# Seven half-size products in place of eight in the gate and up projections of two feed-forwards

## The chip, the core and the metric

The kernel runs on one core of a Trainium2 chip. The metric is the device time in microseconds of one execution, the median of several. Engines are named as the profile names them: PE is TensorE (PEld its weight loads), DVE is VectorE, ACT is ScalarE, POOL is GpSimd, SP issues the weight transfers.

## The reference

Three transformer blocks over 512 tokens of width 1024, in float32, one after the other. The first two end in a feed-forward of hidden width 2816:

```python
def swiglu(h, w_gate, w_up, w_down):
    return (jax.nn.silu(h @ w_gate) * (h @ w_up)) @ w_down
# per layer:
h = rmsnorm(x, ffn_norm[layer])
x = x + swiglu(h, ffn_w_gate[layer], ffn_w_up[layer], ffn_w_down[layer])
```

The third block ends in another feed-forward (`ffn2`) with a convolution, which the change leaves alone.

## The kernel before

All is held with features on the 128 partitions and the 512 tokens along the free axis. Float32 products are made from three fp32r matmuls: a value is split into a high part (ScalarE copies it to fp32r) and a low part (VectorE subtracts the high part from the value), and hi x hi, hi x lo and lo x hi are added up in PSUM. The activations stand split in `XH` and `XL` (8 tiles of 128 features each), multiplied by the norm's gain but not by `rstd`.

Weights come in units of 1 MB: 1024 input features by 256 hidden features, a gate unit and an up unit in turn. SP loads a unit into one of two raw buffers `w_raw` as soon as the low part of the unit two before is made (`w_lo_ready`). ScalarE makes `w_hi` once TensorE has read that buffer's previous weights, VectorE makes `w_lo`, and TensorE (`pair`, line 2893) makes the two 128-feature tiles of the unit, each of 8 x 3 matmuls of 512 columns, in banks 4 and 5 for gate and 2 and 3 for up. A gate and an up unit are one round; there are 11 rounds. The first unit of a feed-forward is made by `first_pair` (line 2839), which follows the norm tile by tile; after it a matmul with ones (line 2410) sums the squares, and ScalarE makes `rstd` (lines 1084 and 1085). VectorE multiplies each tile by `rstd` (lines 1885 and 1900) on its way out of PSUM to `gp` or `ut`, ScalarE applies silu (line 1300), and VectorE multiplies the two into `hid` (line 1912). The order on each engine is the order of the code; rounds 2 to 10 are a hardware loop on PE, ACT, DVE and SP. Then `first_down` (line 2944) and `down_unit` (line 2926) make the down products from `hid`, split again into high and low, in all eight banks.

Other lines that the text names: 1291, 1311 (high parts of up and gate units), 1870, 1876 (their low parts), 1582 and 1036 (low and high parts of other stages' units), 2450 (`token_tile`, 256 columns, in the attention projections), 1970 (an activation times a gain times `rstd`).

Of the kernel before, what the change touches and what calls it, by code (L numbers as in the profile page):

```python
# [8 lines left out]
F32 = mybir.dt.float32  # L9
# [4 lines left out]
ALU = mybir.AluOpType  # L14
# [73 lines left out]
def alibi_rows():  # L88
# [4 lines left out]
    for h in range(4):  # L93
# [10 lines left out]

# [63 lines left out]
def build(nc, d, out, scratch, stages):  # L168
# [18 lines left out]
    with ExitStack() as ctx:  # L187
# [70 lines left out]
        bias_row = sem("bias_row")  # L258
        bias_row_ready = sem("bias_row_ready")
# [9 lines left out]
        sq_mixed = sem("sq_mixed")  # L269
# [5 lines left out]
        gains_ready = sem("gains_ready")  # L275
# [48 lines left out]
        keys_zeroed = sem("keys_zeroed")  # L324
        sb_sum = sem("sb_sum")
# [5 lines left out]
        rope_arg = sem("rope_arg")  # L331
        rope_ready = sem("rope_ready")
        alibi_loaded = sem("alibi_loaded")
        lam_prod = sem("lam_prod")
# [3 lines left out]
        krope_ready = sem("krope_ready")  # L338
# [106 lines left out]
        early_hi, early_lo = (under_arena[:, at:at + 1024].rearrange("p (a b) -> p a b", b=512) for at in early_at)  # L445

# [168 lines left out]
        down_base = {s: KT * i for i, s in enumerate(ffn_order)}  # L615

# [252 lines left out]
        def _(pool):  # L869
# [30 lines left out]
            pool.wait_ge(bias_row_ready, 1)  # L900
# [115 lines left out]
        def _(act):  # L1016
# [263 lines left out]

            def ffn(s):
# [38 lines left out]
                if s != "ffn2":  # L1320
                    up_high(0)
                reciprocal_root(s if s != "ffn2" else "fpre")
                if s == "ffn2":
                    for k in range(2, KT):
                        turned_kept(k)
                body(0)
                if s == "ffn2":
                    body(1)
                with act.Fori(2 if s == "ffn2" else 1, HT // 2 - 1) as i:
                    up_high(i)  # L1330
                    body(i)
                act.wait_ge(hid_done, h0 + 2)
                ffn_hidden_split(s, u0, 0)
                up_high(HT // 2 - 1, last=True)
                body(HT // 2 - 1)
# [15 lines left out]
                if s == "ffn0":  # L1351
                    act.wait_ge(rope_arg, 1)
                    act.activation(rotab[64:128, :], rotab[64:128, :], ACT.Sin).then_inc(rope_ready, 1)
                    exp_and_log()
                if s == "ffn1":
                    act.wait_ge(lam_prod, 1)
# [15 lines left out]
            def mla():  # L1372
# [18 lines left out]
                for half in range(2):  # L1391
# [20 lines left out]
                    if half == 0:  # L1412
                        act.wait_ge(krope_ready, 1)
# [6 lines left out]
            def mix2():  # L1420
                act.wait_ge(gains_ready, 1)
# [146 lines left out]
        def _(dve):  # L1568
# [160 lines left out]
            def even():  # L1729
# [15 lines left out]
                for u in tok_units("even_qkv"):  # L1745
# [34 lines left out]
                    if j == 0:  # L1780
# [7 lines left out]
                        dve.memset(tabx[32:33, :], 1.0).then_inc(bias_row, 1)  # L1788
# [3 lines left out]
                        dve.tensor_tensor(gain12, vec[:, at:at + KT], vec[:, at2:at2 + KT], ALU.mult).then_inc(gains_ready, 1)  # L1792
# [70 lines left out]
            def ffn(s):  # L1863
# [56 lines left out]
                if s == "ffn2":  # L1920
                    body(1)
# [1439 lines left out]
```

## Time and profile before

| | us |
|---|---|
| median of 3 runs | 1924.94 (1923.69 to 1925.65) |
| span of the profiled execution | 1924.0 |
| PE busy | 1890.1 |
| DVE busy | 999.1 |
| ACT busy | 740.1 |
| gate and up work of the first feed-forward, from its second unit on | 228.53 |
| the same of the second | 228.53 |

The profile comes from one execution, whose span is 1924.0 us from the first to the last instruction. "Busy" of PE counts each matmul up to a modelled end, and neighbouring matmuls overlap in it; the time that one matmul costs in a stream is the time from start to start. The view of the chain of waits gives that, as the length of a run of matmuls and their number. Columns of every view are described where it stands first below.

### The profile page before, as it was taken

The page shows a single profiled execution, that of the slowest core. Times are in us where ns is not written, and L with a number is a line of the kernel's source. Part 1 is how long each engine was busy: PE and PEld are TensorE (multiplying, and loading weights), DVE is VectorE, ACT ScalarE, POOL GpSimd, SP SyncE. Part 2 cuts the span into 40 slices and gives each one's busy share as a digit, 9 for nine tenths or more (in the row PEclk, how much of TensorE's full clock was granted, in tenths as well). Part 3 has the DMA queues.
Part 4 walks back from the last instruction along what each step waited for, and adds up shares of the span by engine and source line. Part 5 has one row for each costly group of instructions (what it writes and reads, how often), then busy time and mean ns, then how long its engine had stood idle before and what let it go on. Part 6 is the DMA issues. An engine that isn't in the chain of part 4 may idle for free.

```text
span 1924.0 us, 26779 instructions
## 1 busy us (share of the span) xinstructions
PE 1890.1 (98%) x10729; PEld 1527.6 (79%) x10729; DVE 999.1 (52%) x1418; ACT 740.1 (38%) x1111; POOL 179.1 (9%) x215
## 2 busy tenths in 40 slices
PE   9999999999999999999999999999999999999998
PEld 7875788888888777788888888777878778888887
DVE  5456453434325686553343434749563566656523
ACT  4247432222224575542222323554342454333322
POOL 1001210000001100010000000303551100000001
PEclk9999999999999999999999999999999999999999
DMA  6310133232322202123223232321120223232321
GB/s 201 105 44 1 50 99 98 87 109 87 105 92 80 72 23 66 45 91 105 91 87 109 88 109 87 100 88 44 24 67 25 88 77 109 87 108 89 107 90 66
DMA packets 137795, 158.74 MB, mean 83 GB/s; under 512 B 15976, under 2 KB 125552, under 8 KB 137712
## 3 DMA queue, kind: packets, MB, share of 16 engines
q1 hardware_dynamic: 136272, 155.01, 25.2%
q0 software_dynamic: 1440, 2.58, 0.5%
q8 instruction: 58, 0.95, 0.2%
q14 instruction: 25, 0.20, 0.0%
HBM read 153.89 MB, written 3.68 MB: 82 GB/s over the span
## 4 chain that ended last, share of the span: by engine, by line
PE 90%; DVE 6%; ACT 2%; issue 1%; DMA 0%; SPq 0%; POOL 0%; ACTq 0%; DVEq 0%
PE bank L2893 35%; PE bank L2926 16%; PE bank L2425 13%; PE bank L2450 3%; PE bank L2980 2%; PE bank L2569 2%; PE bank L2944 2%; PE bank L2839 1%; PE bank L2872 1%; PE bank L2597 1%; PE bank L2688 1%; PE bank L2584 1%; PE bank L2511 1%; PE bank L2541 1%; DVE XL L1589 1%
## 5 line engine op out<-in xcount | busy, mean ns | idle before, releaser
L2893 PE MATMUL bank<-XH,w_hi 128*128 128x512 f32 x992 | 386.8, 390 | 0.7 <-DVE arena L1889 0.7
L2893 PE MATMUL bank<-XL,w_hi 128*128 128x512 f32 x992 | 386.0, 389 | 0.0
L2893 PE MATMUL bank<-XH,w_lo 128*128 128x512 f32 x992 | 385.9, 389 | 0.0
L2893 PEld LDWEIGHTS bank<-XH,w_hi 128*128 128x128 f32 x992 | 186.2, 188 | 39.9 <-DVE arena L1889 0.9
L2893 PEld LDWEIGHTS bank<-XL,w_hi 128*128 128x128 f32 x992 | 186.2, 188 | 39.1 <-issue 0.5
L2893 PEld LDWEIGHTS bank<-XH,w_lo 128*128 128x128 f32 x992 | 186.2, 188 | 38.8
L2425 PE MATMUL bank<-XH,w_hi 128*128 128x512 f32 x448 | 178.7, 399 | 2.5 <-DVE w_lo L1582 2.4
L2425 PE MATMUL bank<-XH,w_lo 128*128 128x512 f32 x448 | 175.3, 391 | 0.0
L2425 PE MATMUL bank<-XL,w_hi 128*128 128x512 f32 x448 | 175.1, 391 | 0.0
L1582 DVE TENSOR_TENSOR w_lo<-w_raw,w_hi 128x2048 fp32r<-128x2048 f32 (+5 forms) x67 | 116.4, 1757 | 93.9 <-ACT w_hi L1036 93.5
L1936 DVE TENSOR_TENSOR w_lo<-w_raw,w_hi 128x2048 fp32r<-128x2048 f32 x24 | 55.0, 2292 | 174.2 <-ACT w_hi L1347 174.2
L1036 ACT ACTIVATE w_hi<-w_raw 128x2048 fp32r<-128x2048 f32 (+5 forms) x67 | 96.6, 1464 | 106.8 <-PE bank L2425 44.7
L2926 PE MATMUL bank<-XH,w_hi 128*128 128x512 f32 x320 | 124.5, 389 | 0.0
L2926 PE MATMUL bank<-XH,w_lo 128*128 128x512 f32 x320 | 124.5, 389 | 0.0
L2926 PE MATMUL bank<-XL,w_hi 128*128 128x512 f32 x320 | 124.5, 389 | 0.0
L1900 DVE TENSOR_TENSOR arena<-bank,arena 128x512 f32<-128x512 f32 x66 | 45.5, 690 | 141.0 <-PE bank L2893 141.0
L1291 ACT ACTIVATE w_hi<-w_raw 128x2048 fp32r<-128x2048 f32 x32 | 61.3, 1917 | 147.5 <-PE bank L2893 147.5
L1347 ACT ACTIVATE w_hi<-w_raw 128x2048 fp32r<-128x2048 f32 x24 | 46.0, 1917 | 187.1 <-PE bank L2926 166.5
L1876 DVE TENSOR_TENSOR w_lo<-w_raw,w_hi 128x2048 fp32r<-128x2048 f32 x33 | 75.6, 2290 | 62.9 <-ACT w_hi L1311 56.0
L2425 PEld LDWEIGHTS bank<-XH,w_hi 128*128 128x128 f32 x448 | 84.5, 189 | 25.1 <-DVE w_lo L1582 4.9
L2425 PEld LDWEIGHTS bank<-XL,w_hi 128*128 128x128 f32 x448 | 84.5, 189 | 18.9 <-issue 1.7
L2425 PEld LDWEIGHTS bank<-XH,w_lo 128*128 128x128 f32 x448 | 84.5, 189 | 17.8
(459 smaller groups left out, 3336.1 us busy)
## 6 DMA issues: line engine op xcount, KB each, us to landing
w_raw<-in_ffn_w_gate SPq DMA_DIRECT2D x22, 1024.0 KB, 5.3
w_raw<-in_ffn_w_up SPq DMA_DIRECT2D x22, 1024.0 KB, 5.3
w_raw<-in_ffn_w_down SPq DMA_DIRECT2D x22, 1024.0 KB, 4.9
w_raw<-in_w_up SPq DMA_DIRECT2D x22, 1024.0 KB, 5.1
w_raw<-in_w_in SPq DMA_DIRECT2D x13, 1024.0 KB, 5.3
w_raw<-in_w_down SPq DMA_DIRECT2D x11, 1024.0 KB, 5.0
w_raw<-in_even_w_in SPq DMA_DIRECT2D x8, 1024.0 KB, 5.3
w_raw<-in_even_w_out SPq DMA_DIRECT2D x4, 1024.0 KB, 5.3
```

The source lines that it names most:

```text
L1036: last = act.activation(to, frm, ACT.Copy)
L1291: act.activation(w_hi[:, (u0 + 1) % 2, :], w_raw[:, (u0 + 1) % 2, :], ACT.Copy).then_inc(w_hi_ready, 1)
L1347: act.activation(w_hi[:, slot, :], w_raw[:, slot, :], ACT.Copy).then_inc(w_hi_ready, 1)
L1582: last = dve.tensor_tensor(to, frm, hi.bitcast(F32), ALU.subtract)
L1876: dve.tensor_tensor(w_lo[:, a, :], w_raw[:, a, :], w_hi[:, a, :].bitcast(F32), ALU.subtract).then_inc(w_lo_ready, 1)
L1900: dve.tensor_tensor(to[:, c, :], bank[2 + c][:, :], rstd, ALU.mult).then_inc(u_out, 1)
L1936: dve.tensor_tensor(w_lo[:, slot, :], w_raw[:, slot, :], w_hi[:, slot, :].bitcast(F32), ALU.subtract).then_inc(w_lo_ready, 1)
L2425: m = pe.matmul(bank[to][0:M, :], cols(w, k), x[:, x0 + k, :], start=(first_k and k == 0 and j == 0), stop=(last_k and k == kt - 1 and j = ...
L2450: m = pe.matmul(bank[to][:, 0:N], x[:, x0 + k, s * P:(s + 1) * P], cols(w, k), start=(k == 0 and j == 0), stop=(k == kt - 1 and j == 2))
L2569: pe.matmul(bank[SCORE[g % 4]][:, c:c + P * nk], qc[:, h, P * i:P * (i + 1)], kc[:, h, P * k0:P * (k0 + nk)], start=True, stop=True)
L2893: m = pe.matmul(bank[b][:, :], w[:, k, P * c:P * (c + 1)], x[:, k, :], start=(k == 0 and j == 0), stop=(k == KT - 1 and j == 2))
L2926: m = pe.matmul(bank[p][:, :], left, right, start=False, stop=(stop and c == 1 and j == 2))
```

## The change

In `ffn0` and `ffn1`, rounds 0 and 1 stay as they are. The other 9 rounds, 18 units, are made in another way (the 2x2 block scheme of Strassen in Winograd's form). The unit's weights are seen as four blocks, A11 and A12 (first 128 hidden features; first and second half of the inputs) and A21 and A22 (second 128 hidden features), the activations as four blocks, B11, B12 (first half of the features; first and second 256 tokens), B21 and B22. Seven products m1 to m7, each of 4 row tiles x 3 matmuls of 256 columns, take the place of eight:

- activations once per feed-forward: `xn` = X x gain x rstd (8 DVE operations), differences T1 = B12 - B11, T2 = B22 - T1, T3 = B22 - B12, T4 = B21 - T2 (`difference`, 4 DVE operations of 1024 columns), and high and low parts of seven operands of 1024 columns. Those of m1, m5 and m6 have buffers of their own (`fs_x`); those of m2, m3, m7 and m4 take the place of `XH` and `XL`;
- per unit on DVE (`sums`): S1 = A21 + A22, S3 = A11 - A21, S2 = S1 - A11, S4 = A12 - S2, each of 512 columns; ACT and DVE split A11, A12, A22 (512 columns each) and the pairs S1, S2 and S4, S3 (1024 columns each). Each has one block of 512 columns in `w_hi` and `w_lo`, A22 two in turn;
- m1 = A11 B11, m6 = S2 T2, m7 = S3 T3 and m4 = A22 T4 go into one bank one after the other, and ACT copies that bank out between them (`keep_1`, `keep_2`, `keep_3`); m5 = S1 T1 and m3 = S4 B22 share a second bank (`keep_5` between), m2 = A12 B21 has a third. DVE adds the corners of the result: m2 + m1; m5 + m3 + (m1 + m6); (m1 + m6 + m7) + m5; the fourth is the first bank itself after m4. `rstd` isn't applied again.

TensorE, ACT and DVE run the 18 units as straight code with an order written out. Seven semaphores used once become one counter, `prepared`, to free semaphores. The first down unit takes the output banks in another order and waits for the last silu, corner and hidden tile within it. The core of the diff, with parts left out:

```diff
+        FAST = ("ffn0", "ffn1")
+        FAST_UNITS = HT - 4
+        FAST_BLOCK = {"m1": 4, "m5": 5, "m6": 6, "m2": 7, "m3": 0, "m7": 1}
+        FAST_BANK = ({"a": 4, "b": 5, "c": 6}, {"a": 3, "b": 2, "c": 1})
...
+        def fast_raw(u):
+            r = w_raw[:, u % 2, :].rearrange("p (k n) -> p k n", n=256)
+            return r[:, 0:4, 0:P], r[:, 4:8, 0:P], r[:, 0:4, P:2 * P], r[:, 4:8, P:2 * P]
...
+        def fast_operand(m):
+
+            if m in ("m1", "m5", "m6"):
+                i = ("m1", "m5", "m6").index(m)
+                return fs_x[2 * i], fs_x[2 * i + 1]
+            i = ("m2", "m3", "m7", "m4").index(m)
+            return [x[:, 2 * i:2 * i + 2, :].rearrange("p a b -> p (a b)").rearrange("p (a b) -> p a b", b=256)
+                    for x in (XH, XL)]
+
+        def fast_source(m):
+            b11, b21, b22 = xn[:, 0:4, 0:256], xn[:, 4:8, 0:256], xn[:, 4:8, 256:512]
+            return {"m1": b11, "m2": b21, "m3": b22, "m5": xd[:, 0, :, :], "m6": xd[:, 1, :, :],
+                    "m7": xd[:, 2, :, :], "m4": xd[:, 3, :, :]}[m]
...
+                def high_56(n):
+                    act.wait_ge(fs_sum, fast_sum(s, n, 0))
+                    if n >= 1:
+                        act.wait_ge(fs_done, fast_done(s, n - 1, "m6"))
+                    act.activation(fast_w_pair(w_hi, fast_block(n, "m5")), fs_w[:, 0:2, :, :], ACT.Copy).then_inc(fs_hi, 1)
...
+                fast_operand_high(s, "m5")
+                fast_operand_high(s, "m6")
+                high_1(0)
+                high_56(0)
+                high_2(0)
+                act.wait_ge(u_ready, h0 + 4)
+                fast_operand_high(s, "m2")
+                keep_1(0)
+                high_37(0)
+                keep_5(0)
+                fast_operand_high(s, "m3")
+                for n in range(FAST_UNITS):
+                    if n % 2 == 1:
+                        gate_silu_last(n - 1)
+                    keep_2(n)
+                    if n == 0:
+                        fast_operand_high(s, "m7")
+                        high_1(1)
+                        high_4(0)
+                    if n < last:
+                        high_56(n + 1)
+                        high_2(n + 1)
+                        high_4(n + 1)
+                    else:
+                        u = u0 + HT
+                        loaded(u)
+                        act.wait_ge(fs_done, fast_done(s, n, "m2"))
+                        act.activation(w_hi[:, u % 2, :], w_raw[:, u % 2, :], ACT.Copy).then_inc(w_hi_ready, 1)
+                    keep_3(n)
+                    if n == 0:
+                        fast_operand_high(s, "m4")
+                    if n < last:
+                        high_37(n + 1)
+                        keep_1(n + 1)
+                    if n + 2 <= last:
+                        high_1(n + 2)
+                    if n % 2 == 0:
+                        gate_silu(n)
+                    if n == last - 1:
+                        ffn_hidden_split(s, u0, 0)
+                    if n < last:
+                        keep_5(n + 1)
...
+                def sums(n):
+                    u = u0 + 4 + n
+                    a11, a12, a21, a22 = fast_raw(u)
+                    dve.wait_ge(w_loaded[u % 2], 16 * (u // 2 + 1))
+                    if n >= 1:
+                        dve.wait_ge(fs_lo, fast_split(s, n - 1, "m37"))
+                    links[0] += 1
+                    first_sum = links[0]
+                    dve.tensor_tensor(fs_w[:, 0, :, :], a21, a22, ALU.add).then_inc(dve_link, 1)
+                    dve.tensor_tensor(fs_w[:, 3, :, :], a11, a21, ALU.subtract)
+                    dve.wait_ge(dve_link, first_sum)
+                    dve.tensor_tensor(fs_w[:, 1, :, :], fs_w[:, 0, :, :], a11, ALU.subtract).then_inc(fs_sum, 1)
+                    dve.wait_ge(fs_sum, fast_sum(s, n, 0))
+                    dve.tensor_tensor(fs_w[:, 2, :, :], a12, fs_w[:, 1, :, :], ALU.subtract).then_inc(fs_sum, 1)
...
+                def corner_11(n):
+                    dve.wait_ge((silu_done, hid_done)[n % 2], h0 + 2 * fast_round(n))
+                    dve.wait_ge(fs_done, fast_done(s, n, "m2"))
+                    dve.wait_ge(fs_kept, fast_kept(s, n, "s1"))
+                    dve.tensor_tensor(tile_of(n)[:, 0, 0:256], bank[FAST_BANK[n % 2]["c"]][:, 0:256], fs_s1,
+                                      ALU.add).then_inc(fs_first, 1)
+
+                def corner_12(n):
+                    dve.wait_ge(fs_done, fast_done(s, n, "m3"))
+                    dve.wait_ge(fs_kept, fast_kept(s, n, "s2"))
+                    dve.tensor_tensor(tile_of(n)[:, 0, 256:512], bank[FAST_BANK[n % 2]["b"]][:, 0:256], fs_s2,
+                                      ALU.add).then_inc((g_out, u_out)[n % 2], 1)
+
+                def corner_22(n):
+                    dve.wait_ge(fs_kept, fast_kept(s, n, "s3"))
+                    dve.tensor_tensor(tile_of(n)[:, 1, 256:512], fs_s3, fs_s5, ALU.add).then_inc((g_out, u_out)[n % 2], 1)
...
+                plain_gate(0)
+                up_low_next(0)
+                for k in range(KT):
+                    m = dve.scalar_tensor_tensor(xn[:, k, :], X[:, k, :], gain_of(s, k), rstd, ALU.mult, ALU.mult)
+                m.then_inc(xn_ready, 1)
+                difference(0)
+                plain_up(0)
+                plain_hidden(0)
+                operand_low("m1")
+                up_low(1)
+                difference(1)
+                plain_gate(1)
+                difference(2)
+                difference(3)
+                operand_low("m5")
+                operand_low("m6")
+                sums(0)
+                low_1(0)
+                low_56(0)
+                low_2(0)
+                plain_up(1)
+                operand_low("m2")
+                low_37(0)
+                operand_low("m3")
+                plain_hidden(1)
+                for n in range(FAST_UNITS):
+                    if n == 0:
+                        operand_low("m7")
+                        low_1(1)
+                        low_4(0)
+                    if n < last:
+                        sums(n + 1)
+                    if n >= 1 and n % 2 == 0:
+                        hidden_last(n - 1)
+                    if n == last:
+                        hidden_split(0)
+                    corner_11(n)
+                    if n < last:
+                        low_56(n + 1)
+                        low_2(n + 1)
+                        low_4(n + 1)
+                    corner_12(n)
+                    if n == last:
+                        up_low_next(HT // 2 - 1)
+                    corner_22(n)
+                    if n == 0:
+                        operand_low("m4")
+                    if n < last:
+                        low_37(n + 1)
+                    if n + 2 <= last:
+                        low_1(n + 2)
+                    if n % 2 == 1:
+                        hidden(n)
+                hidden_last(last)
...
+                def product(n, m):
+                    i, kind = fast_round(n), n % 2
+                    to = FAST_BANK[kind][{"m1": "a", "m6": "a", "m7": "a", "m4": "a", "m5": "b", "m3": "b", "m2": "c"}[m]]
+                    pe.wait_ge(xp_lo, fast_x(s, m))
+                    if m == "m1":
+                        pe.wait_ge(fs_lo, fast_split(s, n, "m1"))
+                        if n < 2:
+                            pe.wait_ge((g_out, u_out)[kind], h0 + 4)
+                        else:
+                            pe.wait_ge((silu_done, hid_done)[kind], h0 + 2 * i)
+                    if m == "m5":
+                        pe.wait_ge(fs_lo, fast_split(s, n, "m56"))
+                        if n >= 2:
+                            pe.wait_ge(*fast_out(s, n - 2, 1))
+                    if m == "m6":
+                        pe.wait_ge(fs_kept, fast_kept(s, n, "s1"))
+                    if m == "m2":
+                        pe.wait_ge(fs_lo, fast_split(s, n, "m2"))
+                        if n >= 2:
+                            pe.wait_ge(fs_first, fast_first(s, n - 2))
+                    if m == "m3":
+                        pe.wait_ge(fs_lo, fast_split(s, n, "m37"))
+                        pe.wait_ge(fs_kept, fast_kept(s, n, "s5"))
+                    if m == "m7":
+                        pe.wait_ge(fs_kept, fast_kept(s, n, "s2"))
+                    if m == "m4":
+                        pe.wait_ge(w_lo_ready, u0 + 4 + n + 1)
+                        pe.wait_ge(fs_kept, fast_kept(s, n, "s3"))
+                    b = fast_block(n, m)
+                    hi, lo = fast_w(w_hi, b), fast_w(w_lo, b)
+                    xh, xl = fast_operand(m)
+                    for t in range(4):
+                        for j, (w, x) in enumerate(((hi, xh), (hi, xl), (lo, xh))):
+                            mm = pe.matmul(bank[to][:, 0:256], w[:, t, :], x[:, t, :],
+                                           start=(t == 0 and j == 0 and m in ("m1", "m5", "m2")),
+                                           stop=(t == 3 and j == 2), skip_group_check=True)
+                    if m == "m4":
+                        mm.then_inc(fast_ready(s, n)[0], 2)
+                    else:
+                        mm.then_inc(fs_done, 1)
+
+                def fast_rounds():
+                    product(0, "m1")
+                    product(0, "m5")
+                    for n in range(FAST_UNITS):
+                        for m in ("m6", "m2", "m3", "m7"):
+                            product(n, m)
+                        if n + 1 < FAST_UNITS:
+                            product(n + 1, "m1")
+                            product(n + 1, "m5")
+                        product(n, "m4")
...
-                        for i, p in enumerate((0, 1, 6, 7, 4, 5, 2, 3)):
-                            if c == 0 and i == 6:
+                        for i, p in enumerate((0, 7, 6, 5, 4, 1, 2, 3) if s in FAST else (0, 1, 6, 7, 4, 5, 2, 3)):
+                            if s in FAST and c == 0:
+                                if p == 4:
+                                    pe.wait_ge(silu_done, h0 + HT)
+                                if p == 1:
+                                    pe.wait_ge(fs_first, fast_first(s, FAST_UNITS - 1))
+                                if p == 2:
+                                    pe.wait_ge(u_out, h0 + HT)
+                                if p == 3:
+                                    pe.wait_ge(hid_done, h0 + HT)
```

## Rows read from the trace of the kernel before

**Rows 1.** The page's totals, and two groups: out<-in shape xcount | busy, mean ns | idle
```profile
PE 1890.1 (98%) x10729; PEld 1527.6 (79%) x10729; DVE 999.1 (52%) x1418; ACT 740.1 (38%) x1111; POOL 179.1 (9%) x215
...
L2893 PE MATMUL bank<-XL,w_hi 128*128 128x512 f32 x992 | 386.0, 389 | 0.0
...
L2893 PEld LDWEIGHTS bank<-XL,w_hi 128*128 128x128 f32 x992 | 186.2, 188 | 39.1 <-issue 0.5
```

**Rows 2.** Chain of waits: start us, length us, engine and line, count
```profile
270.20 228.53 PE bank L2893 x1008
498.73 11.20 PE bank L2944 x48
...
851.21 228.53 PE bank L2893 x1008
```

**Rows 3.** Windows: length, busy us (instructions) of each engine, granted clock, DMA share
```profile
core 0: us, PE busy (x) PEld busy (x) DVE busy (x) ACT busy (x) POOL busy (x), PEclk, DMA share, GB/s
270.20:498.70 228.50, 228.50 (x1009) 189.16 (x1009) 90.33 (x86) 57.82 (x49) 0.00 (x0) 1.00 0.31 97
851.20:1079.70 228.50, 228.50 (x1010) 189.16 (x1009) 90.33 (x86) 57.83 (x49) 0.00 (x0) 1.00 0.31 97
```

**Rows 4.** Chain of waits where matmuls of 256 and of 64 columns run
```profile
62.08 11.50 PE bank L2450 x96
...
1353.27 2.87 PE bank L2450 x24
1356.14 2.01 PE bank L3129 x64
```

**Rows 5.** Timeline of PE across two tiles (24 matmuls from 62.0): start, duration
```profile
64.66 0.28 PE L2450 MATMUL bank<-w_lo,XH 128*128 128x256 f32 x1
64.78 0.28 PE L2450 MATMUL bank<-w_hi,XH 128*128 128x256 f32 x1
64.90 0.28 PE L2450 MATMUL bank<-w_hi,XL 128*128 128x256 f32 x1
65.02 0.28 PE L2450 MATMUL bank<-w_lo,XH 128*128 128x256 f32 x1
```

**Rows 6.** Groups on DVE, by shape (columns as in Rows 1)
```profile
L1876 DVE TENSOR_TENSOR w_lo<-w_raw,w_hi 128x2048 fp32r<-128x2048 f32 x33 | 75.6, 2290 | 62.9 <-ACT w_hi L1311 56.0 <-ACT w_hi L1070 6.8
L1582 DVE TENSOR_TENSOR w_lo<-w_raw,w_hi 128x1024 fp32r<-128x1024 f32 x6 | 7.2, 1223 | 5.4 <-ACT w_hi L1036 5.4
L1912 DVE TENSOR_TENSOR arena<-arena 128x512 f32 x52 | 33.4, 684 | 0.0
L2354 DVE TENSOR_TENSOR arena<-arena,bank 128x256 f32<-128x256 f32 x6 | 2.5, 421 | 9.5 <-PE bank L3266 9.5
L1970 DVE SCALAR_TENSOR_TENSOR arena<-arena,vec 128x512 f32<-128x512 f32 x8 | 6.0, 746 | 3.3 <-ACT arena L1085 3.3
```

**Rows 7.** Timeline of DVE, first two rounds of the first feed-forward
```profile
275.89 2.29 DVE L1876 TENSOR_TENSOR w_lo<-w_raw,w_hi 128x2048 fp32r<-128x2048 f32 x1 [2.98 <-ACT w_hi L1311]
278.10 0.68 DVE L1900 TENSOR_TENSOR arena<-bank,arena 128x512 f32<-128x512 f32 x1
281.16 0.69 DVE L1900 TENSOR_TENSOR arena<-bank,arena 128x512 f32<-128x512 f32 x1 [2.38 <-PE bank L2893]
281.77 1.28 DVE L1912 TENSOR_TENSOR arena<-arena 128x512 f32<-128x512 f32 x2
283.12 2.29 DVE L1870 TENSOR_TENSOR w_lo<-w_raw,w_hi 128x2048 fp32r<-128x2048 f32 x1
286.60 0.69 DVE L1885 TENSOR_TENSOR arena<-bank,arena 128x512 f32<-128x512 f32 x1 [1.19 <-PE bank L2893]
292.04 0.69 DVE L1885 TENSOR_TENSOR arena<-bank,arena 128x512 f32<-128x512 f32 x1 [4.75 <-PE bank L2893]
295.24 2.29 DVE L1876 TENSOR_TENSOR w_lo<-w_raw,w_hi 128x2048 fp32r<-128x2048 f32 x1 [2.50 <-ACT w_hi L1311]
```

**Rows 8.** Groups on ACT, by shape
```profile
L1036 ACT ACTIVATE w_hi<-w_raw 128x1024 fp32r<-128x1024 f32 x6 | 6.1, 1050 | 22.4 <-PE bank L2450 22.4
L1349 ACT ACTIVATE XH<-arena 128x512 fp32r x48 | 27.2, 614 | 0.0
L1196 ACT ACTIVATE arena<-bank 128x256 f32<-128x256 f32 x8 | 3.0, 378 | 0.0
```

**Rows 9.** Transfers by group: count, size, us from issue to landing
```profile
w_raw<-in_ffn_w_gate SPq DMA_DIRECT2D x22, 1024.0 KB, 5.3
```

**Rows 10.** A 512-column group on DVE while POOL works
```profile
L2304 DVE TENSOR_TENSOR arena<-arena 128x512 f32<-128x512 f32 x4 | 7.1, 1768 | 0.0
```

More of the change, by code:

```diff
@@ L324, in build @@
         keys_zeroed = sem("keys_zeroed")
+        fs_done = sem("fs_done")
+        fs_hi = sem("fs_hi")
+        fs_lo = sem("fs_lo")
+        fs_sum = sem("fs_sum")
+        fs_kept = sem("fs_kept")
+        fs_first = sem("fs_first")
+        xn_ready = sem("xn_ready")
+        xp_hi = sem("xp_hi")
+        xp_lo = sem("xp_lo")
         sb_sum = sem("sb_sum")
@@ L445, in build @@
         early_hi, early_lo = (under_arena[:, at:at + 1024].rearrange("p (a b) -> p a b", b=512) for at in early_at)
+        xn = hid[:, HT - KT:HT, :]
+        xd = hid[:, 6:HT - KT, :].rearrange("p a b -> p (a b)").rearrange("p (t a b) -> p t a b", t=4, b=256)
+        fs_x = [under_arena[:, fin_at + 1024 * i:fin_at + 1024 * (i + 1)].rearrange("p (a b) -> p a b", b=256)
+                for i in range(6)]
+        fs_w = arena[:, 0:2048].rearrange("p (s a b) -> p s a b", s=4, b=P)
+        fs_s1 = arena[:, early_at[1] + 1024:early_at[1] + 1280]
+        fs_s2 = gp[:, 1, 0:256]
+        fs_s3, fs_s5 = rstd[:, 0:256], rstd[:, 256:512]
         taken[0] = base1
@@ new lines, in fast_split, with fast_kept, fast_sum, fast_first @@
+        def fast_split(s, n, m):
+            return 4 * (FAST_UNITS * FAST.index(s) + n) + ("m1", "m56", "m2", "m37").index(m) + 1
+        def fast_kept(s, n, m):
+            return 4 * (FAST_UNITS * FAST.index(s) + n) + ("s1", "s5", "s2", "s3").index(m) + 1
+        def fast_sum(s, n, pair):
+            return 2 * (FAST_UNITS * FAST.index(s) + n) + pair + 1
+        def fast_first(s, n):
+            return FAST_UNITS * FAST.index(s) + n + 1
+        def fast_x(s, m):
+            return 7 * FAST.index(s) + ("m1", "m5", "m6", "m2", "m3", "m7", "m4").index(m) + 1
@@ L1420, in mix2 @@
             def mix2():
[L1421 removed]
+                act.wait_ge(prepared, PREPARED["gains_ready"])
                 feed("pre")
@@ L2903, in ffn @@
                     pair(0, 1)
-                with pe.Fori(1, HT // 2) as i:
-                    pair(i, 0)
-                    pair(i, 1)
+                    pair(1, 0)
+                    pair(1, 1)
+                    fast_rounds()
+                else:
+                    first_four()
+                    with pe.Fori(1, HT // 2) as i:
+                        pair(i, 0)
+                        pair(i, 1)
                 u0 = first[s + "_down"]
```

251 lines of the change are left out of this document (203 added, 48 removed).

## Prediction

> **What bounds the kernel now.** I read the totals first: TensorE is busy for 1890.1 of 1924.0 us, VectorE for 999.1 [rows 1]. The chain of waits then shows that each of the two feed-forwards the change touches runs its gate and up work from the second unit on as one unbroken run of 1008 matmuls, 228.53 us long, with the down products straight behind it [rows 2]. So what counts is how closely matmuls follow each other. The busy column cannot tell that: it gives 389 ns to each of these matmuls, but 228.53/1008 is 226.7 ns; the ends overlap. I call this start-to-start distance the spacing. In this stretch TensorE has its full granted clock (1.00), VectorE works 90.33 of 228.50 us, ScalarE 57.82, GpSimd nothing [rows 3]. The side engines have room, and any TensorE time taken out comes off the end, unless a side engine becomes late.
>
> **TensorE's work.** A unit is one 1 MB block of weights (256 hidden features). Before it takes 2 x 8 x 3 = 48 matmuls of 512 columns: 48 x 226.7 ns = 10.88 us. After it takes 7 products x 4 row tiles x 3 = 84 matmuls of 256 columns. The streamed columns fall by an eighth, but the matmuls and weight loads rise by three quarters, so all hangs on the spacing at 256 columns. The trace has that shape with the same operand type: runs of 96 in 11.50 us and of 24 in 2.87 us, so 119.7 ns [rows 4]. Starts across the boundary between two 24-matmul tiles there, where a wait and a new accumulation stand, are also 0.12 us apart [rows 5]. Hence 84 x 119.7 = 10.05 us, 0.83 less per unit. There are 18 units per feed-forward: 195.9 - 181.0 = 14.9 us, twice, 29.8 us. Bounds of the spacing: below, half of 226.7, 113.4 ns, as no matmul can stream fewer columns; above, 226.7. I take 119.7, the row of the very shape.
>
> **The code without its hardware loop.** 1512 matmuls in a row now come as straight code. A straight stretch of 64 small matmuls runs at 2.01/64 = 31 ns each [rows 4], four times the density wanted here, without a pause. I cost it at nothing; a pause of 1 us per 15 us would cost 24 us in all.
>
> **VectorE per unit.** It does four block sums and differences of 512 columns, low parts of 3 x 512 and 2 x 1024 columns, three corners of 256 and, per pair of units, one hidden product of 512 and two of 256. Durations: 2.29 us for 2048 columns, 1.22 for 1024, 0.69 for 512, 0.42 for 256 [rows 6]. Two in a row take 1.28, not 1.37, so the spacing of the wide ones is 0.60, and for the others about 0.08 less than the duration [rows 7]. Sum: 2.4 + (1.8 + 2.3) + 1.0 + 0.65 = 8.2, plus 0.2 for the two sums that wait for the one before: 8.4 us of 10.05. ScalarE, with the same 0.08 off its durations: 3 x 0.53 + 2 x 0.97 for the high parts, four copies out of PSUM at 0.30, half of the silus, about 5.3 us [rows 8]. Both fit.
>
> **Do the waits fit too?** One unit on TensorE goes m6, m2, m3, m7, m1 and m5 of the next unit, m4; each is 1.44 us. The tightest weights are those of m5: their block is free only after m6 (1.44), ScalarE makes the high pair (1.05) while VectorE waits for m2 to end (2.9, plus 0.2 for the result to arrive), makes the first corner and then the low pair (1.2), done at about 4.7; m5 starts at 7.2. That is 2.5 us to spare. The pair for m3 and m7 has its block after m7 (5.75), and goes through a copy, the high pair and the low pair to 8.6; m3 starts at 12.9. Copies of bank a have 2.9 us each. VectorE's odd units carry the hidden products and end about 0.7 us late, which the next even unit takes back. So I expect no wait in the steady part. If VectorE stopped being covered, each microsecond of its list above 10.05 costs 36 us.
>
> **Transfers.** One 1 MB load per 10.05 instead of 10.88 us; it lands in 5.3 us [rows 9], and its buffer is free one unit earlier than it is needed. Nothing.
>
> **The start of each feed-forward** is where it costs. I walk it in the first one. New on VectorE before the first fast product: the normalised activations (8 x 0.67), four differences and the low parts of m1, m5, m6 (seven of 1024 columns, 1.14 each), the first sums and low parts. In the rows of before VectorE idles 2.38, 1.19, 4.75 and 2.50 us between its jobs of these two rounds [rows 7], and more behind them. Laid end to end from 278.2, where the second gate's low part ends: activations to 283.5, first difference 284.7, up and hidden products 287.2, low m1 288.3, second up's low part 290.5, difference 291.7, gate products 292.9, differences 295.2, low m5 and m6 297.4, sums 300.0, low parts of the first unit 302.3. TensorE ends the second round at 302.7, so m1 and m5 start on time, with 2 us to spare. The operands of m2, m3, m7 and m4, though, lie in the buffers that the second round still reads, and can be made only after 302.7, 1.05 us on ScalarE and 1.14 on VectorE each, among the other work. VectorE reaches low m2 at 305.2, m3 at 308.4 (in time), the hidden products 309.6, low m7 at 310.8, where TensorE stands ready at 309.9: 0.9 us. Behind it come two low parts, the second unit's sums (313.8), ScalarE's pair (314.9) and the low pair at 316.1, where m5 could start at 313.6: 2.5 us. Then two low parts, two corners and low m4 at 319.1, wanted at 317.6: 1.6 us. From there VectorE gains on TensorE. At the end m4 of the last unit has no m1 and m5 ahead of it and waits 0.6 us for the copy after m7; the down products are reordered so that what is late comes last, and their weights are ready 0.5 us before. Waits together: 5.6 us per feed-forward. Bounds: zero, if all of this hid; 8 us, if no VectorE operation overlaps the one before it.
>
> Here the trace is to be held against a page. The pairs of 512-column operations take 1.28 us against 2 x 0.684 [rows 7]: the next one starts before the first has ended. The Trainium skill (VectorE: DVE Perf Modes, "The DRAIN you can't avoid") says that the next operation does not start until the pipe empties; taken as full durations this gives about 7.9 us of waits per feed-forward and an end at 1911 us. The rows speak for the overlap.
>
> **Edits at nothing.** Seven semaphores folded into one counter: the same increments in the same order, all set long before they are awaited. The rstd factor leaves the fast units because it is now in the activations; that work is counted above.
>
> **Sum.** 2 x (5.6 - 14.9) = -18.6; 1924.0 - 18.6 = 1905.4 us for the profiled execution's span, which lies 0.9 under the median 1924.94 of the runs; so 1906.3 us.
>
> **Rivals.** (a) Slower: the weight load of a product's first matmul is no longer hidden. A load takes 188 ns [rows 1], more than the 119.7 of a half-size matmul, and the two overlap only while loads can be issued ahead; a load behind a wait at a product's head could stand bare. There are 252 products; 0.19 us each gives 48 us, 1954 us. It decides from 18.6/252 = 0.074 us per product, or from a mean spacing of 125.9 ns, 5% above the row. Against it: rows 5. Only the length of the products (12, not 24) and the number of waits at their heads are new. Chance 0.07. Spacing that falls less than in proportion is also what a page has: the Trainium skill (TensorE: Matmul & The Clock Gate, "Back-to-back issue gap") gives about 81 ns at 128 columns and 131 at 512 for a stream of load and matmul pairs; by its ratio at 256 a unit would grow, and the time would be near 2050 us. The rows, 226.7 and 119.7, do not fit it. Chance 0.02.
> (b) VectorE becomes the bound. Its operations on half-row views of the raw weights have no row of before; with GpSimd beside it 512-column operations took up to 1.77 us [rows 10]. GpSimd rests here, but if the list grew by 30%, to 10.9 us, the units would be as long as before, and with the waits at the start the time is about 1937. It reaches no change at 10.4 us. Chance 0.05.
> (c) The waits at the start are hidden after all: 1924.9 - 29.8 = 1895 us. Against it stands the order of the operand parts above. Chance 0.04.
> (d) Small waits in every unit that my walk misses, 0.3 to 0.5 us: 1917 to 1924 us. For it: every engine's list is one fixed order with a wait in nearly every entry. Chance 0.12.
>
> **Chances and range.** The forecast holds 0.70, within 1900 to 1912 (waits of 3 to 9 us per feed-forward, spacing within 1 ns). A range of 0.8 takes in most of (d): 1899 to 1918. Changes under 0.2%, 3.9 us, cannot be told from none. Faster takes the forecast, (c) and most of (d): 0.85; same 0.05; slower 0.10.
>
> **What would show it.** Right: 1512 matmuls of 128x256 per feed-forward at 119 to 120 ns; three waits of 1 to 3 us on VectorE's low parts in the first 20 us after the second round, none in the steady part; the first down product 9 us earlier within its stage. VectorE about 85% busy there. Wrong: products that start late by a steady amount, VectorE without idle time, or idle time of TensorE with no releaser.

## The result and the profile after

The changed kernel takes 1905.65 us, median of 4 runs (1903.98 to 1905.95), against 1924.52; ratio 0.9897, interval 0.9885 to 0.9909. The forecast was 1906.3.

The page's totals of the changed kernel, for those of [rows 1]:

```profile
span 1902.2 us, 30229 instructions
PE 1861.4 (98%) x12025; PEld 1565.1 (82%) x12025; DVE 1187.0 (62%) x1798; ACT 867.0 (46%) x1431; POOL 178.9 (9%) x215
```

TensorE has 1296 matmul records more and 29 us less to do; VectorE has 188 us more, and the time still fell. The chain of waits of the first feed-forward, where [rows 2] had one run of 1008 (start us, length us, what, count):

```profile
256.41 10.89 PE bank L3227 x48
...
268.16 32.69 PE bank L3281 x144
300.85 2.81 PE bank L3320 x24
...
311.72 1.06 ACT w_hi L1386
312.81 1.08 DVE w_lo L2151
...
315.90 1.15 DVE XL L2114
317.09 167.87 PE bank L3320 x1404
...
485.57 1.67 PE bank L3320 x12
487.25 11.20 PE bank L3396 x48
```

Rounds 0 and 1 are as before (32.69/144 = 227 ns). Between 303.7 and 317.1 the chain leaves TensorE for ScalarE and VectorE (the list is cut here): the start of the fast units is where TensorE is late. Then come 1404 matmuls with no step of another engine. The same feed-forward before began at

```profile
258.45 10.89 PE bank L2839 x48
```

From the first unit's start to the first down product it is 487.25 - 256.41 = 230.84 us, before 498.73 - 258.45 = 240.28; in the second feed-forward 230.40 against 240.27. These two stretches hold 19.3 of the 21.8 us between the two profiled spans. A further 2.0 lies ahead of the first feed-forward, in work that did not change; the starts of that stage range from 256.41 to 259.18 us over all kernels profiled here, and in the window 210 to 220 us the clock was 0.86 before and 1.00 after. The down products and the attention stages between the feed-forwards are as long as before (340.74 and 340.76 us), so nothing was handed back there. From the second feed-forward's first down product to the end it is 843.79 us, before 844.26; over all kernels that were timed this last part, which no run changed, takes 842.92 to 844.26. Differences of 1 us at the end, and of nearly 3 us ahead of the first feed-forward, say nothing about a change.

What TensorE waited for in the second feed-forward (waiting line, releaser, us in total, times, longest):

```profile
PE bank L3320 <- DVE w_lo L2151: 2.3, 1, 2.3
PE bank L3320 <- DVE XL L2114: 1.9, 2, 1.3
PE bank L3320 <- ACT arena L1410: 0.6, 1, 0.6
```

These are m5 of the second unit, m7 and m4 of the first, and m4 of the last: the four places of the forecast. In steady state VectorE repeats itself every 10.00 us (start us, duration, first corner of units 2 and 3):

```profile
332.17 0.42 DVE L2167 TENSOR_TENSOR arena<-bank,arena 128x256 f32<-128x256 f32 x1
...
342.17 0.42 DVE L2167 TENSOR_TENSOR arena<-bank,arena 128x256 f32<-128x256 f32 x1 [1.39 <-PE bank L3320]
```

The 1.39 is VectorE waiting for TensorE: it has time to spare. Over a long window (length, busy us of PE, PEld, DVE, ACT, POOL, clock, DMA share):

```profile
330.00:480.00 150.00, 150.00 (x1262) 150.00 (x1261) 126.82 (x202) 85.98 (x160) 0.00 (x0) 1.00 0.34 106
```

VectorE is at 126.82/150 = 85%, for a forecast of 84 to 85%.

One thing had not been foreseen. The clock of TensorE around the longest wait in the first feed-forward (length, busy us of PE, clock, DMA share, GB/s):

```profile
313.00:314.00 1.00, 0.00 (x0) 1.00 1.09 388
314.00:315.00 1.00, 0.82 (x6) 0.83 0.65 214
315.00:316.00 1.00, 1.00 (x6) 0.50 0.06 16
...
317.00:318.00 1.00, 0.91 (x4) 0.50 0.89 285
318.00:320.00 2.00, 2.00 (x18) 0.98 0.99 346
```

After standing still for 2.3 us (until 314.2), TensorE runs at 0.50 of its clock, 1.2 GHz, for about 3.5 us. In the second feed-forward of this execution it did not fall, behind the same 2.3 us.

### The profile page after: what moved, and what is told of

The parts are those of the page before. It is cut to its first block, busy times and chain, and to the rows that moved or that the text cites. A ratio compares the mean times of both kernels' runs of the same rounds, so it can differ in the third digit from the quotient of the medians.

```text
span 1902.2 us, 30229 instructions
## 1 busy us (share of the span) xinstructions
PE 1861.4 (98%) x12025; PEld 1565.1 (82%) x12025; DVE 1187.0 (62%) x1798; ACT 867.0 (46%) x1431; POOL 178.9 (9%) x215
## 4 chain that ended last, share of the span: by engine, by line
PE 89%; DVE 7%; ACT 3%; issue 1%; POOL 0%; ACTq 0%; DVEq 0%
PE bank L3320 18%; PE bank L3369 17%; PE bank L3281 15%; PE bank L2813 14%; PE bank L2838 3%; PE bank L3432 2%; PE bank L2957 2%; PE bank L3396 2%; PE bank L3227 1%; PE bank L3260 1%; PE bank L2985 1%; PE bank L3076 1%; PE bank L2972 1%; PE bank L2899 1%; PE bank L2929 1%
## 5 line engine op out<-in xcount | busy, mean ns | idle before, releaser
L2813 PE MATMUL bank<-XH,w_hi 128*128 128x512 f32 x448 | 179.0, 399 | 2.6 <-DVE w_lo L1798 2.5
L2813 PE MATMUL bank<-XH,w_lo 128*128 128x512 f32 x448 | 175.1, 391 | 0.0
L2813 PE MATMUL bank<-XL,w_hi 128*128 128x512 f32 x448 | 175.1, 391 | 0.0
L3320 PE MATMUL bank<-XH,w_hi 128*128 128x256 f32 x576 | 164.0, 285 | 4.2 <-DVE XL L2114 3.0
L3281 PE MATMUL bank<-XH,w_hi 128*128 128x512 f32 x416 | 162.7, 391 | 0.7 <-DVE arena L2276 0.7
L3320 PE MATMUL bank<-XL,w_hi 128*128 128x256 f32 x576 | 163.0, 283 | 0.0
L3320 PE MATMUL bank<-XH,w_lo 128*128 128x256 f32 x576 | 163.0, 283 | 0.0
L3281 PE MATMUL bank<-XH,w_lo 128*128 128x512 f32 x416 | 161.9, 389 | 0.0
L3281 PE MATMUL bank<-XL,w_hi 128*128 128x512 f32 x416 | 161.9, 389 | 0.0
L3320 PE MATMUL bank<-under_arena,w_hi 128*128 128x256 f32 x864 | 157.0, 281 | 4.7 <-DVE w_lo L2151 4.7
L3320 PEld LDWEIGHTS bank<-under_arena,w_hi 128*128 128x128 f32 x864 | 133.4, 189 | 5.2 <-issue 5.0
L3369 PE MATMUL bank<-XL,w_hi 128*128 128x512 f32 x320 | 124.5, 389 | 0.0
L3369 PE MATMUL bank<-XH,w_hi 128*128 128x512 f32 x320 | 124.5, 389 | 0.0
L3369 PE MATMUL bank<-XH,w_lo 128*128 128x512 f32 x320 | 124.5, 389 | 0.0
L3320 PEld LDWEIGHTS bank<-XH,w_hi 128*128 128x128 f32 x576 | 110.2, 191 | 5.7 <-DVE XL L2114 3.9
L3320 PEld LDWEIGHTS bank<-XL,w_hi 128*128 128x128 f32 x576 | 110.5, 192 | 0.0
```

What stands on the lines that cost most here:

```text
L2813: m = pe.matmul(bank[to][0:M, :], cols(w, k), x[:, x0 + k, :], start=(first_k and k == 0 and j == 0), stop=(last_k and k == kt - 1 and j = ...
L3281: m = pe.matmul(bank[b][:, :], w[:, k, P * c:P * (c + 1)], x[:, k, :], start=(k == 0 and j == 0), stop=(k == KT - 1 and j == 2))
L3320: mm = pe.matmul(bank[to][:, 0:256], w[:, t, :], x[:, t, :], start=(t == 0 and j == 0 and m in ("m1", "m5", "m2")), stop=(t == 3 and j == ...
L3369: m = pe.matmul(bank[p][:, :], left, right, start=False, stop=(stop and c == 1 and j == 2))
```

## Experiments

All kernels that were timed were timed beside the kernel before on the same chip. Theory: the gain is the columns of the dropped product less the cost of half-size matmuls, less the waits at the start; VectorE is just covered. Rivals: the heads of the products cost something, straight code costs or gains something, VectorE already binds.

**Half-size matmuls alone.** The kernel before, all else kept (the start and stop flags of the call are left out here):

```diff
+for h in ((slice(0, 256), slice(256, 512)) if s != "ffn2" else (slice(0, 512),)):
     for k in range(KT):
         for j, (w, x) in enumerate(((hi, XH), (hi, XL), (lo, XH))):
-            m = pe.matmul(bank[b][:, :], w[:, k, P * c:P * (c + 1)], x[:, k, :],
+            m = pe.matmul(bank[b][:, h], w[:, k, P * c:P * (c + 1)], x[:, k, h],
```

> The kernel before, with every matmul of 512 columns in the gate and up tiles of the first two feed-forwards (all but the first unit of each) made as two of 256 columns, and eight products' worth of work kept. Nothing changes on the side engines. My account: a matmul of 512 columns costs 226.7 ns from start to start and one of 256 costs 119.1 ns, so a unit goes from 48 x 226.7 = 10.88 us to 96 x 119.1 = 11.43 us, 0.55 us more, 42 times: 23.2 us slower, about 1948. If half-size matmuls were free of extra cost (113.4 ns) the time would not move, 1925. If products of 12 matmuls behind waits had paid more than long runs, this kernel, whose runs are 24 long, would show a smaller spacing than the changed kernel's 119.1 ns: below 118 ns, under 1943.

Measured: 1949.78 us, ratio 1.0131 (1.0114 to 1.0147). Its chain:

```profile
268.39 241.91 PE bank L2894 x2016
```

241.91/2016 = 120.0 ns; before, 228.53 us for the same work, so 13.4 us more per feed-forward, 0.64 per unit. The spacing here, in tiles of 24, is not smaller than in the products of 12 with all their waits, which with the same buffers `XH` and `XL` as moving operand are also 120 ns apart: the heads, on which rival (a) rested, cost nothing. The size costs and the dropped product pays: a unit goes 10.88 to 11.52 (half size), from there to 10.08 by one product less in eight, and the other 0.08 comes with the operands in buffers of their own (see Spacing below).

**Straight code alone.** The kernel before, in the first two feed-forwards (the branch that keeps the loop for `ffn2`, and the wait that now has to know a round by its number, are left out here):

```diff
-with pe.Fori(1, HT // 2) as i:
+for i in range(1, HT // 2):
     pair(i, 0)
     pair(i, 1)
```

> The kernel before, with TensorE's hardware loop over the rounds of the first two feed-forwards written out as straight code (960 matmuls each), nothing else changed. My account gives straight code no cost: 1924.5, within 0.2% (1921 to 1928). If the fetch of straight code stalled TensorE, the rounds would be longer than 21.76 us; 1 us in each of 20 would give 1945. If the loop's branch cost something that the change took away, it would be faster by up to a few us, and part of the gain would be the loop's and not the product's.

Measured: 1924.19 us, ratio 0.9994 (0.9985 to 1.0004); the run of 1008 is 228.53 us long again, in both feed-forwards:

```profile
269.40 228.53 PE bank L2893 x1008
```

Straight code neither costs nor gains.

**How far VectorE is from binding.**

```diff
+for _ in range(1):        # 3 in the second kernel
+    link(dve.tensor_tensor(fs_w[:, 3, :, :], a11, a21, ALU.subtract))
 dve.tensor_tensor(fs_w[:, 3, :, :], a11, a21, ALU.subtract)
```

> The changed kernel, with one more VectorE operation of 512 columns in the block sums of every fast unit (the difference A11 - A21 made twice, the second after the first has ended). It adds 0.72 us to VectorE's list, from 8.45 to 9.2 us per unit of 10.0. My account: the steady units stay at 10.0 us, and only the second unit's sums, which TensorE waits for at the start, are 0.72 us later: 1.5 us more in all, 1907. If VectorE already bound the units, all 36 would be longer: up to 26 us more, 1931.

> The same with three more operations per unit: VectorE's list becomes 8.45 + 2.2 = 10.6 us, more than TensorE's 10.0. My account: now VectorE sets the unit. A walk through the orders gives a pair of units 21.1 to 21.3 us long in place of 20.0, with TensorE waiting once in each pair, before m1 of an up unit, for the hidden product of the up unit before; with the start that is 23 us over the changed kernel, about 1929, so slower than the kernel before. If VectorE had more room than its list says, the time would stay near 1910.

Measured: 1907.87 us with one (ratio 0.9909, 0.9892 to 0.9925), 1925.68 with three (1.0004, 0.9994 to 1.0013). With one, the 1404 matmuls still run without a step of another engine:

```profile
318.89 167.57 PE bank L3322 x1404
```

With three, TensorE waits once in each pair of units for the hidden product, as expected:

```profile
381.02 0.36 PE L3322 MATMUL bank<-under_arena,w_hi 128*128 128x256 f32 x1 [0.77 <-DVE arena L2194]
402.02 0.36 PE L3322 MATMUL bank<-under_arena,w_hi 128*128 128x256 f32 x1 [0.76 <-DVE arena L2194]
```

A pair of units now takes 21.0 us, 10.5 each, and VectorE is busy 19.69 of 20.00 us. So VectorE had about 1.5 us per unit to spare, the first 0.72 are free in the steady units, and 2.2 us eat the whole gain. Rival (b) was wrong about the kernel and about right on the price: with a list of 8.45 + 2.2 = 10.65 us its 36 us for each us above 10.05 give 22, and 20 were measured. Its point of no change, 10.4 us, does not follow from that price (18.6/36 above 10.05 is 10.57); the run met it at 10.65.

**Fewer columns still.**

```diff
-mm = pe.matmul(bank[to][:, 0:256], w[:, t, :], x[:, t, :],
+mm = pe.matmul(bank[to][:, 0:128], w[:, t, :], x[:, t, 0:128],
```

> The changed kernel, with every matmul of the seven products cut to 128 columns: half of the columns of each product are left out, with all weight loads, waits and side work kept. Two questions. (1) The spacing within a product: if it is the columns at full clock plus the same 13 ns, 53 + 13 = 66 ns; if a weight load sets a floor, more (by the 81 ns that the Trainium skill, TensorE: Matmul & The Clock Gate, Back-to-back issue gap, gives for 128 columns, it would be 81). (2) VectorE's own pace: TensorE needs only 5.6 us per unit at 66 ns, so VectorE's list of 8.45 us sets the unit. A walk through the orders gives 16.7 us for a pair of units in place of 20.0, 58 us off in all, about 1847. If TensorE still bound the units, 20 us and more would come off beyond that. If some side operation waited more than I think, the time would be above 1865.

This kernel leaves out half of every product. Measured: 2172.25 us (one run), 267 slower than the changed kernel instead of 58 faster: my expectation failed on a thing I had not asked about, the clock. While it was 1.00, starts were 0.11 us apart; at 311.6 us it fell, and stayed down until the 512-column down products (620 us). Windows on both sides of the fall, PE alone:

```profile
302.00:306.00 4.00, 4.00 (x38) 1.00 0.00 0
...
311.00:311.50 0.50, 0.50 (x7) 1.00 0.45 39
311.50:312.00 0.50, 0.25 (x3) 0.57 0.56 127
...
314.00:318.00 4.00, 3.60 (x16) 0.50 0.50 143
```

And the waits of TensorE around the falls, first in this feed-forward and then in the second, where the clock fell between 1014 and 1016 us:

```profile
308.83 0.33 PE L3320 MATMUL bank<-XH,w_hi 128*128 128x128 f32 x1 [0.79 <-DVE XL L2114]
314.29 0.66 PE L3320 MATMUL bank<-under_arena,w_hi 128*128 128x128 f32 x2 [2.53 <-DVE w_lo L2151]
...
1014.21 0.33 PE L3320 MATMUL bank<-XH,w_hi 128*128 128x128 f32 x1 [0.79 <-DVE XL L2114]
```

So this kernel's clock was down before the wait of 2.5 us began, and within the second feed-forward no wait ahead of the fall was longer than 0.8 us. A long wait is not what brought it down here.

And of all engines, to and across the start of the down products:

```profile
500.00:620.00 120.00, 119.38 (x561) 119.22 (x560) 54.10 (x84) 38.70 (x68) 0.00 (x0) 0.50 0.18 56
620.00:640.00 20.00, 20.00 (x84) 16.29 (x84) 7.41 (x7) 5.92 (x6) 0.00 (x0) 0.95 0.32 113
```

At 0.50 the matmuls of 128 columns start 213 ns apart (559.82 to 561.10 us for six). The same kernel at 192 columns:

> The changed kernel with every matmul of the seven products cut to 192 columns, a quarter of each product left out. With 128 columns the spacing was 111 ns where the clock was still at 1.00 and 213 ns after it had fallen to 0.50 for good, against 119 to 120 at 256 columns. Columns alone would give 80 + 13 = 93 ns here at full clock. If a weight load sets a floor of 111 ns, the spacing is 111 ns here too while the clock is at 1.00. If the clock holds throughout, the units are 84 x 111 = 9.3 us and about 1880 results; if it falls to 0.50 as with 128 columns, 213 ns and over 2150.

Measured: 1887.34 us (one run; a quarter of every product is left out), 7 above the expected 1880, the clock at 1.00 in the steady part, and starts 0.11 us apart:

```profile
360.08 0.27 PE L3320 MATMUL bank<-XH,w_hi 128*128 128x192 f32 x1
360.19 0.27 PE L3320 MATMUL bank<-XL,w_hi 128*128 128x192 f32 x1
360.31 0.27 PE L3320 MATMUL bank<-XH,w_lo 128*128 128x192 f32 x1
...
361.09 0.27 PE L3320 MATMUL bank<-XH,w_hi 128*128 128x192 f32 x1
```

The last is the ninth after the first: 1.01/9 = 112 ns. With 128 columns it was 113 (four spacings from 305.04 to 305.49). There is a floor of about 112 ns under a load and matmul pair at full clock. It does not depend on the columns, which fits the weight load; but the issue of the two instructions was kept as well, and no run parts them. At 0.50 the pair takes 213 ns with 128 columns and also with 256, as the second profile of the changed kernel shows (1.07 us for five):

```profile
320.48 0.41 PE L3320 MATMUL bank<-XH,w_hi 128*128 128x256 f32 x1
...
321.55 0.41 PE L3320 MATMUL bank<-XH,w_lo 128*128 128x256 f32 x1
```

The half-size matmuls of the change sit 7 ns above the floor. Halving the blocks once more, for another eighth off the columns, would not pay: an estimate from the floor is 147 matmuls at 112 ns, 16.5 us a unit against 10.00. The Trainium skill (TensorE: Matmul & The Clock Gate, "Back-to-back issue gap") says that the spacing is set by the load and the matmul together; these runs fit that for narrow matmuls, but the floor is 112 ns where it has 81 at 128 columns.

The 128-column kernel could not tell VectorE's own pace any more; the pair with three more operations did.

**The order at the start.** On VectorE and ScalarE, for the first two fast units alone (the places that the moved calls leave are not shown):

```diff
 operand_low("m3")
+operand_low("m7"); low_1(1); sums(1); low_4(0); low_56(1); operand_low("m4")
+corner_11(0); corner_12(0); corner_22(0); low_2(1)
 plain_hidden(1)
+low_37(1); low_4(1); low_1(2)
-for n in range(FAST_UNITS):
+for n in range(1, FAST_UNITS):
...
 high_4(0)
+fast_operand_high(s, "m4")
...
 keep_1(n + 1)
+if n == 0: keep_5(1)
```

> The changed kernel with another order at the start of the fast units alone: VectorE makes the low operand of m7, the second unit's sums and low pair before the hidden product of round 1 and the first unit's corners; ScalarE makes the high operand of m4 before the second unit's high pair, and the copy after the second m5 before the silu. The same operations, none left out. In the changed kernel TensorE stands 0.7, 2.3 and 0.4 to 1.3 us before m7, m5 and m4, behind VectorE. A walk through the new order leaves one wait of 2.0 us before m5 and 0.5 before the next unit's m5: 2.5 us less per feed-forward, 5 us in all: 1900.6 against 1905.6. If the waits at the start are not set by VectorE's order, nothing moves. In the first feed-forward the clock fell to 0.50 for 3.5 us after the longest of these waits; a shorter wait should keep it at 1.00.

> The changed kernel itself, on the same chip as the two above and timed as often: 1905.6 us, a ratio of 0.990 to the kernel before. In its profile: units of 10.0 us, three waits of TensorE at the start of each feed-forward, and the question whether the clock falls to 0.50 after the longest of them again.

Measured: 1899.17 us (1898.39 to 1900.02), ratio to the kernel before 0.9864 (0.9848 to 0.9881); the changed kernel beside it 1905.32 (1903.79 to 1909.93), 0.9895 (0.9879 to 0.9912). The new order is 6.2 us faster than the change and beats both kernels. What TensorE still waits for in each feed-forward:

```profile
PE bank L3328 <- DVE w_lo L2152: 1.8, 1, 1.8
PE bank L3328 <- ACT arena L1410: 0.6, 1, 0.6
PE bank L3328 <- issue: 0.2, 1, 0.2
```

The stretch from first unit to first down product is 227.76 us, 2.6 less than the 230.40 of the changed kernel without a fall of the clock; the walk had 2.5. Twice that is 5.3 of the 6.2 us between the medians. The profiles place 0.6 to 0.9 more in the last part, from the second feed-forward's first down product on, which is the same code (842.92 us with the new order, 843.54 and 843.79 in the two profiles of the changed kernel); it is not shown that the order did that. The clock adds to the difference where it falls. In the second profile of the changed kernel it fell in both feed-forwards and for longer, and the stretches are 232.76 and 232.74 us:

```profile
318.00:320.00 2.00, 0.97 (x4) 0.50 0.69 193
320.00:322.00 2.00, 2.00 (x12) 0.50 0.92 325
322.00:324.00 2.00, 2.00 (x11) 0.50 0.02 7
324.00:328.00 4.00, 4.00 (x34) 0.96 0.00 0
```

With the new order it stayed at 1.00 in both stretches.

**Is it the standing still?** The changed kernel with TensorE given useless work in its longest wait:

```diff
+if (n, m) == (1, "m5"):
+    for _ in range(20):
+        pe.matmul(bank[7][:, 0:256], fs_x[0][:, 0, 0:P], fs_x[0][:, 1, :], start=True, stop=True)
 pe.wait_ge(xp_lo, fast_x(s, m))
```

> The changed kernel with 20 extra matmuls of 256 columns, about 2.4 us, into a bank that nobody reads, ahead of the second unit's m5, in the place where TensorE stands 2.3 to 3 us for VectorE. In the changed kernel's profiles the granted clock fell to 0.50 after this wait in three of the four feed-forwards looked at, for 3.5 to 7 us; in the kernel with the other order at the start, whose wait is 1.8 us, it stayed at 1.00. If the wait brings the clock down, the filled one keeps 1.00, and extra work makes the kernel faster: up to 2.3 us per feed-forward where the clock fell, 1901 to 1904 against 1905.3. If the clock falls for another reason, the clock still falls to 0.50 about 314 to 320 us, and the time is 1905 to 1907.

Measured: clock 1.00 at the place in both feed-forwards, though the 1.3 us wait before m4 remained (its start in the record):

```profile
319.87 0.38 PE L3323 MATMUL bank<-XH,w_hi 128*128 128x256 f32 x1 [1.27 <-DVE XL L2114]
```

Both stretches are 230.41 us, 2.3 less than where the clock fell for long. But the time is 1905.84 us (1904.96 to 1907.08), ratio 0.9897, no better than the changed kernel's 1905.32 to 1905.65, and not the 1901 to 1904 that I expected. So the profiles bear out that filling the wait keeps the clock up, in two feed-forwards of one execution against three falls in four, and a worth in the median is not shown. The record gives a reason why it may be small: the mean clock of each run stands there too. It was 0.993 in the profiled run of 1909.93 us, whose two falls held 13.8 us, and 0.995 or 0.996 in the other three runs. A difference of 0.003 over 1904 us is, as an estimate, 11 us less at half the clock, so most runs of the changed kernel seem to have had one short fall or none.

## Why the prediction was right, step by step

- **Spacing.** 119.7 ns was taken from a row of the same shape; the steady unit is 10.00 us, 119.0 ns. That made 1.0 us more per feed-forward than the sum had. The difference between operands is visible in the profile: three matmuls take 0.355 us where the moving operand is in its own buffers (m1, m5, m6) and 0.36 where it lies in `XH` and `XL`, as all of [rows 4] do. The half-size kernel, all on `XH` and `XL`, has 120.0. Why is open.
- **Waits at the start.** Walked at 5.6 us. From the stretch: 240.28 less 18 x 10.88 (the slow units) and plus 18 x 10.00 leaves 224.4, so 230.4 has 6.0 us of waits. (The list of waits shows 4.8, because it counts from the end of the last matmul, 0.36 us after its start, and not from 0.12; four places make 1.0 more.) The places and releasers were the ones named; m5 of the second unit first, 2.3 against 2.5. The wait before m7 was 0.65 us, shorter than the 1 to 3 us that were named as the sign.
- **No waits in the steady part.** Right; and the margin of VectorE, 10.0 less 8.45 us, was measured by filling it. ScalarE's list was put at 5.3 us and took 85.98/150, 5.7 per unit, with room to spare as well.
- **VectorE's operations overlap.** Lists of 512-column operations start 0.60 us apart (309.79, 310.39, 310.99), as [rows 7] had it; with full durations the kernel would by the prediction's walk be some 5 us slower (2 x 2.3). The page that the prediction holds against this, the Trainium skill (VectorE: DVE Perf Modes, "The DRAIN you can't avoid"), adds in the same paragraph that a next operation that is not held starts earlier. So the overlap need not contradict the page, and 1911 us is what the sentence without its exception would give.
- **Edits at nothing.** Straight code was tested alone and is free. The folded semaphores and the order of the first down products were not tested apart; no wait shows at either.
- **The sum.** 2 x 9.3 was forecast. With the clock at 1.00 it is 240.28 - 230.40 = 9.9 per feed-forward. The fall of the clock takes 0.4 to 2.4 us of that back in some executions; the prediction had no term for it. The profiled span is 1902.2 us, 3.2 under the 1905.4 that the sum gives: 0.7 of that lies in the two stretches, 2.0 ahead of the first feed-forward and 0.5 behind, in work that did not change. The nearness of 1906.3 to the median 1905.65 is thus in part luck: the spacing was 1.0 us per feed-forward too long, the waits 0.4 too short, the clock was left out, and the unchanged parts vary by more than the miss.
- **The rivals.** (a) fell with the half-size kernel, whose long runs are spaced no closer. What stood behind (a), that something other than the columns can bound the spacing, is true 7 ns further down; that this is the weight load fits, but is not shown. (b) would have come in from about 1.5 us more per unit on. (c) was half right: order does hide a part of the waits, 2.6 us per feed-forward, but nobody had written that order. (d) did not occur.

## What to carry to other kernels

A scheme that drops products pays only as long as its smaller matmuls stay above the floor that the spacing has (here 112 ns, reached at 192 columns): look for a row of the very shape and operand type, and take the start-to-start distance, not the duration. Then walk the in-order lists of the side engines through the first units, not only the steady one: there the setup work and the first outputs meet, and an order made for the steady state costs several us. And look at the granted clock around the waits of TensorE, not only at the waits: the loss after one can be as large as the wait (2.4 us behind 2.3), and a cut in columns can bring the clock down without a long wait and cost more than it saves.

## What the runs showed of the hardware that was not expected

- At full clock a load and matmul pair with 128x128 fp32r weights takes 112 to 113 ns with 128 and with 192 columns, 118 to 120 with 256, 226.7 with 512; at 0.50, 213 ns with 128 and with 256 columns.
- The clock fell to 0.50 at TensorE's longest wait (2.3, 3.1 or 4.5 us), in three cases before the wait had ended and in four up to 1.5 us behind it, in seven of the eight feed-forwards of the kernels with 256-column products that kept that wait: the two profiles of the changed kernel (three of four) and those with one and with three more VectorE operations (four of four). It stayed there for 3.5 to 7 us. It did not fall behind 1.8 us (the new order), nor where the 2.3 us were filled. The 192-column kernel fell behind 2.5 us and came back as well. With 128 columns it fell behind a wait of only 0.8 us, and did not come back for 300 us, though TensorE was busy all the time. So the waits alone do not decide it. Why one fall in eight is missing, and what makes the clock recover, is open.
